# First stage reordered around its modulation units, and twelve slots for the weights beside the first attention

## The reference

```python
c_act = jax.nn.silu(c)[:, None, :]
cc_act = jax.nn.silu(c_ctx)[None, None, :]
for i in range(DEPTH):
    mx = jnp.split(c_act @ ada_w[i] + ada_b[i], 6, axis=-1)
    mc = jnp.split(cc_act @ ada_w[i] + ada_b[i], 6, axis=-1)
    h_x = modulate(rms_norm(x, norm1_g[i]), mx[0], mx[1])
    h_c = modulate(rms_norm(y_ctx, norm1_g[i]), mc[0], mc[1])
    # i == 0: windowed attention of x over ctx and x, 16 heads, softmax with a sink
    # i == 1: retention in both directions
    x = x + mx[2] * out_x
    x = x + mx[5] * swiglu(modulate(rms_norm(x, norm2_g[i]), mx[3], mx[4]), ffn_w_in[i], ffn_w_out[i])
```

## Time and profile before

| | us |
|---|---|
| median of 3 runs | 2638.8 (2636.25 to 2638.82) |
| the profiled execution, whole | 2634.45 |
| its span, first to last instruction | 2632.6 |
| PE busy over the span | 2511.2 (95%) |
| DVE busy | 1526.1 (58%) |
| ACT busy | 1266.5 (48%) |
| mean granted clock of PE | 0.98 |
| transfers | 398.25 MB, 151 GB/s |

### The profile page before, as it was taken

The page is one execution under the profiler, slowest core; times in us unless marked ns, Lnnn a source line. Parts: engine busy times, 40 slices in busy tenths (PEclk is TensorE's granted clock), DMA queues, the critical chain, the costliest instruction groups (busy, mean ns, idle before and its releaser), DMA issues.

```text
span 2632.6 us, 42437 instructions
## 1 busy us (share of the span) xinstructions
PE 2511.2 (95%) x15422; PEld 2133.2 (81%) x15422; DVE 1526.1 (58%) x2429; ACT 1266.5 (48%) x1950; POOL 133.8 (5%) x108
## 2 busy tenths in 40 slices
PE   5999999999999998999999999999999999999998
PEld 3735577888878995788888999898888899989887
DVE  2435535333235336666677665768767766576774
ACT  1426633222224343455555458655555545864553
POOL 3000000000000000000000002110000000211000
PEclk8969999999999999999999999999999999999999
DMA  8228742332223341465565555446656455544663
GB/s 262 72 82 269 252 127 74 99 98 92 88 84 120 96 135 49 138 195 180 182 183 162 182 176 159 144 145 191 188 178 190 151 188 171 171 140 146 187 182 121
DMA packets 398654, 398.25 MB, mean 151 GB/s; under 512 B 17361, under 2 KB 396769, under 8 KB 398545
## 3 DMA queue, kind: packets, MB, share of 16 engines
q1 hardware_dynamic: 395680, 390.25, 47.9%
q0 software_dynamic: 2864, 6.57, 0.8%
HBM read 395.72 MB, written 1.05 MB: 151 GB/s over the span
## 4 chain that ended last, share of the span: by engine, by line
PE 79%; DVE 6%; ACT 5%; issue 5%; DMA 3%; POOL 2%; SPq 0%; ACTq 0%; DVEq 0%; POOLq 0%
PE acc L813 27%; PE acc L807 24%; PE acc L809 12%; PE acc L792 4%; DMA raw<-in_ada_w_dram 3%; DVE w_lo L1728 2%; ACT w_hi L1187 2%; PE acc L869 1%; PE wk L936 1%; PE wk L1025 1%; PE wk L963 1%; PE wk L888 1%; PE acc L1156 1%; POOL XC L738 1%; PE wk L878 1%
## 5 line engine op out<-in xcount | busy, mean ns | idle before, releaser
L1728 DVE TENSOR_TENSOR w_lo<-raw,w_hi 128x1024 fp32r<-128x1024 f32 (+1 forms) x656 | 815.7, 1257 | 624.5 <-ACT w_hi L1187 623.2
L1187 ACT CAST w_hi<-raw 128x1024 fp32r<-128x1024 f32 (+1 forms) x656 | 670.2, 1033 | 460.1 <-PE acc L813 229.5
L813 PE MATMUL acc<-h_all,w_hi 128*128 128x256 f32 (+1 forms) x3360 | 747.7, 318 | 20.7 <-DVE w_lo L1728 6.6
L807 PE MATMUL acc<-h_all,w_hi 128*128 128x512 f32 x2016 | 710.4, 397 | 4.5 <-DVE h_all L1837 4.5
L813 PEld LDWEIGHTS acc<-h_all,w_hi 128*128 128x128 f32 x3360 | 561.0, 192 | 65.4 <-issue 14.9
L809 PE MATMUL acc<-h_all,w_lo 128*128 128x256 f32 x2016 | 566.5, 281 | 0.0
L813 PE MATMUL acc<-h_all,w_lo 128*128 128x256 f32 (+1 forms) x1680 | 533.9, 318 | 0.0
L807 PEld LDWEIGHTS acc<-h_all,w_hi 128*128 128x128 f32 x2016 | 379.5, 188 | 93.5 <-issue 4.7
L809 PEld LDWEIGHTS acc<-h_all,w_lo 128*128 128x128 f32 x2016 | 382.6, 190 | 0.2
L813 PEld LDWEIGHTS acc<-h_all,w_lo 128*128 128x128 f32 x1680 | 322.4, 192 | 20.9
L807 PE MATMUL acc<-hid_all,w_hi 128*128 128x512 f32 x880 | 312.4, 398 | 2.9 <-DVE w_lo L1728 2.9
(11 more groups left out here) (342 smaller groups left out, 2498.0 us busy)
## 6 DMA issues: line engine op xcount, KB each, us to landing
raw<-in_w_in_dram SPq DMA_DIRECT2D x100, 512.0 KB, 4.1
raw<-in_ada_w_dram SPq DMA_DIRECT2D x96, 512.0 KB, 5.1
raw<-in_ffn_w_in_dram SPq DMA_DIRECT2D x88, 512.0 KB, 3.6
raw<-in_ffn_w_gate_dram SPq DMA_DIRECT2D x88, 512.0 KB, 3.9
raw<-in_ffn_w_up_dram SPq DMA_DIRECT2D x88, 512.0 KB, 4.0
raw<-in_ffn_w_down_dram SPq DMA_DIRECT2D x80, 512.0 KB, 4.2
raw<-in_ret_w_qkvg_dram SPq DMA_DIRECT2D x48, 512.0 KB, 3.6
raw<-in_ffn_w_out_dram SPq DMA_DIRECT2D x40, 512.0 KB, 3.6
```

The source lines that it names most:

```text
L807: pe.matmul(o, w_hi[:, s, k, c], merged[:, :, kk, t], start=(u == 0 and k == 0), stop=False, skip_group_check=True)
L813: mm = pe.matmul(o, ws[:, s, k, c], xs[:, kk, t], start=(u == 0 and k == 0 and i == 0), stop=(last and k == nk - 1 and i == 2))
L1187: act.copy(w_hi[:, s, 0:nk, :], raw[:, s, 0:nk, :]).then_inc(hi_done, 1)
L1728: dve.tensor_tensor(w_lo[:, s, 0:nk, :], raw[:, s, 0:nk, :], w_hi[:, s, 0:nk, :], ALU.subtract).then_inc(lo_done, 1)
```

## The change

The 16 units of `ada0a` get buffers of their own: eight in what will be `w_hi` and `w_lo` (`ring` is laid over `raw`, `w_hi` and `w_lo`, twelve slots), eight in an unused part of the arena (`ada_in`). SP issues them all without waiting, and q0's first four units behind them. PE does its first stage in another order, with norms and turnings between the groups of four units; the transposition of parameters goes behind `q0`, and PE waits for the copies. ACT and DVE follow; three of q0's splits move between the deviations and the normed chunks. POOL loads the tokens first and holds `alibi`, `slopes` and the constants of the attention back until the 16 units have been used. The chain on 24 columns moves behind the first attention. The 80 units of `ada0b` and `ada1` go through the twelve slots of `ring` (four are filled as kv0's splits are done, eight as PE has used kv0's units). The diff, cut to its core:

```diff
+RINGED = ADA
+RING = 3 * SLOTS
...
+        with ExitStack() as on:
+            ring = sb("ring", [P, RING, KCH, COLS], F32, on)
         raw = sb("raw", [P, SLOTS, KCH, COLS])
...
-        nf, nf_c, rows_c, prm_rows, _, ada_s = arena(
+        nf, nf_c, rows_c, prm_rows, ada_in, _, ada_s = arena(
...
+            ("ada_in", [P, 2 * SLOTS, KCH, COLS], F32), ("ada_skip", [P, 2 * FC * 2 * S - 6 * D - 6 * D - 4 * P - 2 * SLOTS * KCH * COLS], F32), ("ada_s", [P, 6 * D], F32))
...
+        first_load = [sem(f"first_load{k}") for k in range(4 * SLOTS)]
+        ring_load = [sem(f"ring_load{k}") for k in range(RING)]
...
+        def first_unit(k):
+            return ring[:, SLOTS + k] if k < 2 * SLOTS else ada_in[:, k - 2 * SLOTS]
...
+                        if held in ADA and name == "q0":
+                            held = None
...
+            def side_stream(src):
+                kv, first = J["kv0"], J[SIDE[0]].unit0
+                for k in range(SIDE_UNITS):
+                    name, it, p = side_unit(k)
+                    if k < SLOTS:
+                        sp.wait_ge(lo_done, kv.split(None, kv.iters - 1, k) + SLOTS + 1)
+                    elif k < RING:
+                        sp.wait_ge(units_used, kv.unit(None, kv.iters - 1, k % SLOTS) + SLOTS + 1)
+                    else:
+                        sp.wait_ge(units_used, first + k - RING + SLOTS + 1)
+                    sp.dma_start(ring[:, k % RING], src[name](None, it, p)).then_inc(ring_load[k % RING], 16)
...
-            stream("ada0a", plain(a["ada_w"][0], DC, 0, 2 * D))
+            first_units = plain(a["ada_w"][0], DC, 0, 2 * D)
+            for k in range(4 * SLOTS):
+                sp.dma_start(first_unit(k), first_units(None, k // SLOTS, k % SLOTS)).then_inc(first_load[k], 16)
             wqkv = a["attn_w_qkv"][0]
             stream("q0", plain(wqkv, DC, 0, D))
             stream("kv0", plain(wqkv, DC, D, 512))
-            stream("ada0b", plain(a["ada_w"][0], DC, 2 * D, 4 * D))
-            stream("ada1", plain(a["ada_w"][1], DC))
+            side_stream({"ada0b": plain(a["ada_w"][0], DC, 2 * D, 4 * D), "ada1": plain(a["ada_w"][1], DC)})
...
-            for name, t in (("sel", sel), ("ones", ones)):
-                pool.dma_start(t[:, :], const(name)).then_inc(in_ones, 16)
             tokens(rows, a["x"], in_x)
+            pool.dma_start(ones[:, :], const("ones")).then_inc(in_ones, 16)
             tokens(rows_c, a["ctx"], in_c)
-            for name, t in (("alibi", alibi), ("slopes", slopes)):
-                pool.dma_start(t[:, :], const(name)).then_inc(in_const, 16)
+            pool.dma_start(sel[:, :], const("sel")).then_inc(in_ones, 16)
...
+            pool.wait_ge(units_used, J["ada0a"].unit(None, J["ada0a"].iters - 1, J["ada0a"].body - 1) + SLOTS + 1)
+            for name, t in (("alibi", alibi), ("slopes", slopes)):
+                pool.dma_start(t[:, :], const(name)).then_inc(in_const, 16)
             pool.dma_start(headsum[:].rearrange("p c h -> p (c h)"), const("headsum")).then_inc(in_attn, 16)
...
-                pe.wait_ge(load[p % SLOTS], job.loaded(None, it, p))
+                if name in SIDE:
+                    n = job.unit(None, it, p) - J[SIDE[0]].unit0
+                    landed = ring[:, n % RING]
+                    pe.wait_ge(ring_load[n % RING], 16 * (n // RING + 1))
+                else:
+                    n = it * job.body + p
+                    landed = first_unit(n)
+                    pe.wait_ge(first_load[n], 16)
                 for k in range(KCH):
-                    mm = pe.matmul(acc[32 * k:32 * k + 32, b % 2, 0, 0:S], c_wide[:, u * KCH + k, :], raw[:, p % SLOTS, k, :],
+                    mm = pe.matmul(acc[32 * k:32 * k + 32, b % 2, 0, 0:S], c_wide[:, u * KCH + k, :], landed[:, k, :],
...
-            for it in range(2):
+            banks = [wk[:, 0], wk[:, 1], wk[:, 2], acc[:, 0, 1]]
+            def modulation_units(it):
                 for p in range(J["ada0a"].body):
                     modulation_unit("ada0a", it, p)
-            turn_in(rows, in_x, [wk[:, 0], wk[:, 1], wk[:, 2], acc[:, 0, 1]])
-            turn_in(rows_c, in_c, [wk[:, 0], wk[:, 1], wk[:, 2], acc[:, 0, 1]])
-            for it in range(2, J["ada0a"].iters):
-                for p in range(J["ada0a"].body):
-                    modulation_unit("ada0a", it, p)
+            def turn_units(it):
+                for c in range(4 * it, 4 * it + 4):
+                    mm = turn_chunk("ada0a", c, wk[:, 0, 2 * c:2 * c + 2])
+                return mm
+            modulation_units(0)
+            turn_in(rows, in_x, banks)
+            modulation_units(1)
+            turn_in(rows_c, in_c, banks)
+            pe.wait_ge(in_ones, 16 * 2)
+            pe.wait_ge(prm_ok, 1)
+            norm(0, 0)
+            modulation_units(2)
             pe.wait_ge(x_done, X_START)
-            pe.wait_ge(in_ones, 16 * 2)
-            for c in range(12):
-                turn_chunk("ada0a", c, wk[:, 0, 2 * c:2 * c + 2])
-            norm(0, 0)
             norm(1, 1)
-            for c in range(12, 16):
-                mm = turn_chunk("ada0a", c, wk[:, 0, 2 * c:2 * c + 2])
-            mm.then_inc(ada_sum, 1)
+            for it in range(3):
+                turn_units(it)
+            modulation_units(3)
+            turn_units(3).then_inc(ada_sum, 1)
+            both = slice(0, 2 * S)
+            product("q0", tok=both, normed=(0, 8))
             pe.wait_ge(in_prm, 16 * PRM_DMAS)
             pe.wait_ge(mod_ok, 1)
             turn_parameters(wk[:, 0], range(1, 4))
-            both = slice(0, 2 * S)
-            product("q0", tok=both, normed=(0, 8))
+            pe.wait_ge(prm_ok, 3)
...
-            head("q0")
-            pair_deviations(0, 0)
+            pair_deviation(0)
+            step("q0", None, None, 0, 0)
+            pair_high(0, 0, beside=lambda half, c: step("q0", None, None, 0, 2 * half + c // 3) if (half, c) in ((0, 3), (1, 0)) else None)
             rest("q0", q0)
-            act.wait_ge(soft_v, 1)
-            act.activation(soft_e[:], soft_t[:], ACT.Exp).then_inc(soft_a, 1)
             head("kv0", None, "q0", q0)
...
             attention("first", heads_first(), None, beside_first, SIDE_TURNS)
+            act.wait_ge(soft_v, 1)
+            act.activation(soft_e[:], soft_t[:], ACT.Exp).then_inc(soft_a, 1)
             head("wo0")
...
+            banks = [wk[:, 0], wk[:, 1], wk[:, 2], acc[:, 0, 1]]
             ada(0)
+            turned_in(0, 0, banks)
             ada(1)
-            inputs()
-            for it in range(2, J["ada0a"].iters):
-                ada(it)
-            head("q0")
+            turned_in(4, 1, banks)
+            ada(2)
             def first_modulations():
+                ada(3)
                 dve.wait_ge(ada_sum, 1)
                 modulations(1, 0, wk[:, 0, 0:32].rearrange("p (c w) -> p c w", w=2), 0, 16)
-            pair_norm(0, gain_at(0, 0), 0, before=first_modulations)
+                step("q0", None, 0, 0)
+            pair_norm(0, gain_at(0, 0), 0, before=first_modulations,
+                      beside=lambda half, c: step("q0", None, 0, 2 * half + c // 4) if (half, c) in ((0, 4), (1, 1)) else None)
+            rest("q0", None)
             dve.wait_ge(prm_t, 2)
             dve.tensor_copy(prm[:, 1:3, 0:CUR], wk[:, 0, P:3 * P].rearrange("p (t n) -> p t n", t=2)[:, :, 0:CUR]).then_inc(prm_ok, 1)
             dve.tensor_copy(prm[:, 3, 0:PRM3], wk[:, 0, 3 * P:3 * P + PRM3]).then_inc(prm_ok, 1)
+            head("kv0", None, "q0", None)
+            rest("kv0", None)
...
-            rest("q0", None)
-            dve.wait_ge(soft_a, 1)
...
-            head("kv0", None, "q0", None)
-            rest("kv0", None)
...
             head("wo0")
+            dve.wait_ge(soft_a, 1)
+            n = [1]
+            def chained(ins):
+                ins.then_inc(soft_ok, 1)
+                n[0] += 1
+                dve.wait_ge(soft_ok, n[0])
...
+            chained(dve.tensor_scalar(lam_s[:, :, 1, :], lam, -16.0, None, ALU.mult))
```

68 lines of the change are left out of this document (36 added, 32 removed).

## The result

| | before | after |
|---|---|---|
| median, us | 2637.53 (2636.25 to 2638.82, 4 runs) | 2605.95 (2602.64 to 2607.67, 4 runs) |
| profiled execution, us | 2634.45 | 2607.67 |
| its span, us | 2632.6 | 2605.9 |

The ratio is 0.9879, with a 95% interval of 0.9862 to 0.9896. The direction and the places of the gain were right. The two large terms of the sum, the first stage and the attention, were too small, and two prices that seem right in this one execution are partly luck, as the experiments show.

A forecast was written before the change was run, and what follows sets the result against it. Taken as bounds: weights up to 46 us, a serial chain to 66.3 us, waits for modulation weights in the first attention. 17.2 - 4.0 + 12 - 0.2 = 25.0 us gained, giving 2613.8 us; range 2606 to 2628.

The forecast's parts named there:

- Arrival of the weights: First stage: with 16 units queued, unit 7 arrives at about 23 us and unit 15 at 33 us, not 46.
- PE's chain: First stage: units, norms and turnings on PE end at 45 us, bounds 41 and 57; first normed chunk 19.6 us earlier.
- The chunks: Normed chunks before q0's second block: two splits between them add 3.4 us on DVE; the block begins 17.2 us earlier.
- The hand-over: Between q0 and kv0: PE waits for turnings, copies and a split, 3.0 us, plus 1 for low clock; 4.0 us lost.
- The attention: First attention: the 11.6 us of waits for modulation weights go; gain 12 us, bounds 8 and 15.
- The small chain and the constants: 25 dependent operations moved behind three splits of wo0, and constants loaded later: hidden, zero cost apart from about 0.2 us.
- (a): First stage: PE stays at the low clock, chain ends at 57 us; 13 us gained in all, 2625.8 us; chance 0.15.
- (b): First stage: 16 queued units share the engines, the first complete only at 33 us; 9 us gained, 2629.8 us; chance 0.05.
- (c): First attention: ACT takes over as what PE waits for, 3 of 12 us remain; 2622.8 us; chance 0.11.
- (d): After q0: new idle time drops the clock through kv0, costing 23 us on top of (a); 2649 us; chance 0.03.

The follow-up runs named there:

- e2: The changed kernel with four slots instead of twelve for the modulation units beside the first attention; 2613.3 us, ratio 0.9917.
- e5: The changed kernel with only four of the first stage's unit loads in flight instead of all 16 queued; 2608.2 us, ratio 0.9880.
- e7: The changed kernel with q0's third split behind the 16 normed chunks instead of between them; 2606.9 us, ratio 0.9865.
- e8: The changed kernel with the head norms' second matmul contracting over all 128 rows, 108 of them zeros, instead of 20; 2588.7 us, ratio 0.9800.
- e6: The changed kernel with PE and DVE in the old first-stage order, all 16 units still queued in their own buffers; 2613.1 us, ratio 0.9884.
- e1: The changed kernel run once more without an edit; 2602.8 us, ratio 0.9874.

## Where the prediction was right and where it failed

The time forecast was 2613.8 us and the measured median 2605.95. By stages up to wo0, without the loop, the gain was 30.3 us where 25.0 were forecast. Two steps failed: the low clock put into PE's chain of the first stage, and what a wait for a weight costs in the attention.

**What bounds it.** Right. The two stages named carried the gain: the first stage 24.7 us, the attention 14.2.

**Arrival of the weights.** Right as far as it is seen: unit 7 (the eighth) was forecast for 23 us and used at 22.94, and after it PE waits for none. The later arrivals stay hidden behind PE.

**PE's chain, the first mis-sized term.** It ends at 40.0 us where 45 was taken; the lower bound was 41. The step that failed is the mixture of clock levels, a term of 4 us. The first norm was put "mostly at the low clock (5.5)" and took 3.62, in every one of the ten executions traced with the new order; units 12 to 15 were put "partly low again" and took 1.9 instead of 3.1 us; the last turnings, 1.2 instead of 2. With ctx 0.4 us early these are 4.3 of the 5 us, the rest is small change. The sum "at the full clock", 21.1 us from 17.7 us on, was the better estimate: with the one wait of 1.06 us it ends at 39.9. The bound of 41 was too late because the wait for unit 7 was taken at some 2 us. From 20 us on no gap of PE was longer than 1.06 us, and in "after" it kept the full clock to the end. For the norm that is shown; for units 12 to 15 it is luck, since they took 1.9 us in six of those ten executions and 2.9 to 3.5 in four (e2, e5, e7, e8).

**The chunks, the second.** DVE's part was right: from 41.65 to 58.7 us, 17.06, against 17.25 forecast. What failed is "PE then follows by one chunk (about 1 us instead of 2)": it followed by 3.3, as the third split let PE idle 1.52 us and the low clock behind that (56.2 to 59.7 us) cost as much again. e7 shows both together: without the split in the middle the stretch is 3.0 us shorter.

**The hand-over.** 4.1 us against 4.0. The place was right, the copies and the split are what PE waits for; the number is partly luck. Its parts in "after" are the turnings 0.55, the wait 1.83 and a start of kv0 at the low clock, 1.6, for which 1 was taken. Six of nine executions have no such start, and the hand-over then costs 2.5 us, under the 2.6 to 3.2 of the forecast without it.

**The attention.** 14.2 against 12, within 8 to 15. The waits left entirely, 11.6 us, and with them 2.7 more where the 12 that I took left 0.4. Here the mechanism was wrong, not only the size: the low clock that I saw behind two waits is in "after" as well (0.97 against 0.98, the line at 301.59 us), and the waits cost more than their length since they parted units that PE takes faster in a row (41.2 against 37.5 us of busy time for the same units). ACT and DVE did not become the bound: 1.7 us of waits for `probs_t`, as before.

**The small chain and the constants.** No trace of them in PE's waits: the wait for wo0's first split is 3.1 us, 3.0 before.

**Sum.** 24.7 - 4.5 - 4.1 + 14.2 is 30.3 us where the forecast had 25.0, next to the 31.6 of the medians. The 3.0 us of the loop belong to the executions and not to the change, and the -6.6 behind wo0 are within what executions differ by.

**Rivals.** (a) *Low clock in the first stage* fell as a whole: the units behind the norms took 0.5 us each in "after". Up to 17.5 us it was so: single units took 1.08 us behind waits of 4.39, 0.99 and 0.42 us. The rule of the Trainium skill cited there ("TensorE: Matmul & The Clock Gate") agrees with that start and not with what followed. In e6 single units behind waits of 0.53 to 0.93 us ran at the full clock (0.64 us, the line at 36.21), and in e7 four units ran low with no wait before them (3.52 us). What decides between the two is not shown. (b) *Shared engines* fell: with 16 queued the second unit was in use at 13.8 us, not 33. This agrees with the Trainium skill, "DMA: Bandwidth & Descriptors", section "Queues, rings and completion order", by which an engine takes a ring's descriptors in their order. (c) *Waits change their name* fell, see above. (d) *Slower* fell; its start was there (kv0's first unit took 7.29 us in "after", 5.7 in e1), yet the clock rose again within that unit.

**The range.** Its lower end, 2605, was put together from bounds of single terms and closed to 2606. It lacked two things: the bound of 41 us was itself too late, and the median, which moves by 1 to 3 us between sets of runs of one kernel (2602.8 and 2605.95 here), had no part in it. The 4.35 us that I carried from the profiled execution to the median did not carry either: with four runs the median before lies 3.1 above its profiled execution, and after it lies 1.7 below. By profiled executions the gain is 26.8 us, near the forecast of 25.0 only because 6.6 us were lost behind wo0, against 3.0 won by chance in the loop.

## What to carry to other kernels

When a low clock is put into a sum, look up the same group of work in several executions before giving it one length: the first norm kept its full-clock length in ten of ten, the last four units in six of ten, and the low start of kv0 came in three of nine. One profile shows none of this. A wait can cost more than its length even at an unchanged clock, where it parts work that the engine takes faster in a row. A stage that PE fills without idle time isn't therefore at its limit: look at the granted clock of it as well; here 15 to 18 us lay in a loop that neither the change nor the prediction had looked at. To hide loads, so many slots are enough as leave no wait: here eight did what twelve do.

## What the runs showed of the hardware

PE stayed at the low level of its clock through most or all of a loop in which it was busy 37.28 of 37.59 us, in nine of ten executions in which half of its larger matmuls contracted over 20 rows; with 128 rows, 108 of them zeros, it had risen by the third pair (1.02 us at 139.22), and the loop was at 22.2 to 23.1 us in four of four executions. In the tenth, e2, the clock rose in the middle of the loop and stayed up with 20 rows (granted 1.00 from 153 to 166 us). So 20 rows made the rise late or kept it away; they did not pull a high clock down. The Trainium skill, "TensorE: Matmul & The Clock Gate", section "Why this matters for your kernels", says that one matmul over 32 rows takes the same time as one over 128. At one level of the clock the trace agrees: the shortest single one took 0.587 us with 20 rows and 0.592 with 128. What it adds is that the level differed: a pair took 2.07 us, not 1.02. Why 20 rows keep the clock low is not shown. That it was the rows, and nothing beside the loop, is, as the edit changes little else (a fill by POOL and a wait of ACT for it) and acts alike in both kernels.

The other surprise is how far executions of the same code differ: the stretch behind wo0, with the same matmuls, took 2288.1 to 2298.4 us in the traced executions. A step worth 1 to 3 us is not shown by medians of five runs; it is shown by its place in the trace, and then only where several executions agree on it.
